# Context rows of the second block made inside the last FFN, keys projected first, late conditioning chunks and gate rows moved

## The reference, cut to what matters

```python
mod  = silu(c)     @ ada_w + ada_b      # sh1, sc1, g1, sh2, sc2, g2
modc = silu(c_ctx) @ ada_w + ada_b      # only sh1c, sc1c are needed
u  = rmsnorm(x,   norm1_g) * (1 + sc1)  + sh1
uc = rmsnorm(ctx, norm1_g) * (1 + sc1c) + sh1c
# token mixer: chunked mLSTM with gates in two directions (q of u; k, v, gates of u and uc),
# then differential attention (q of u; k, v of u and uc), merged with two gates, times w_out
x = x + g1 * y
x = x + g2 * moe_ffn(rmsnorm(x, norm2_g) * (1 + sc2) + sh2)   # 32 experts, top 4
return rmsnorm(x, final_norm_g)
```

## Time and profile before

| what | us |
|---|---|
| median of 3 runs | 2032.08 (2030.83 to 2032.79) |
| profiled execution | 2036.05, its span 2034.3 |
| PE / DVE / ACT busy | 1921.2 / 986.6 / 639.7 |
| POOL busy | 10.3 (24 instructions, nearly all DMA issues) |
| last FFN | about 444 to 632 |
| begin of block 2 to the gates mg | 632 to 685 |
| mLSTM heads | about 744 to 866 |
| attention heads | about 866 to 980 |
| merge, w_out, router | about 980 to 1113 |
| experts | from about 1113 |

### The profile page before, as it was taken

One profiled execution on the slowest core, in us unless ns is written; L12 is line 12 of the kernel. 1 busy time (PEld: TensorE's weight loads), 2 busy tenths in 40 slices (PEclk: granted clock), 3 DMA queues, 4 the chain that ended last, 5 costly groups with the idle time before them and its releaser, 6 DMA issues.

```text
span 2034.3 us, 26514 instructions
## 1 busy us (share of the span) xinstructions
PE 1921.2 (94%) x10854; PEld 1280.8 (63%) x10854; DVE 986.6 (48%) x1679; ACT 639.7 (31%) x1074; POOL 10.3 (1%) x24
## 2 busy tenths in 40 slices
PE   8999999999998998999999999999999888999997
PEld 8979998979997787877897333333333333333332
DVE  6888788878877577666655211111111111111112
ACT  5565556565556332355543100000000000000001
POOL 0000000010000000000000000000000000000000
PEclk9999999999999999999999999999999999999999
DMA  8346554446554542422458999999999999999997
GB/s 339 118 184 222 208 184 169 157 159 261 209 186 166 187 175 104 128 101 83 145 201 328 407 416 431 430 433 433 432 431 430 432 431 431 433 433 432 431 430 309
DMA packets 48621, 590.94 MB, mean 290 GB/s; under 512 B 5584, under 2 KB 6288, under 8 KB 17360
## 3 DMA queue, kind: packets, MB, share of 16 engines
q1 hardware_dynamic: 46752, 584.13, 71.1%
q0 software_dynamic: 1488, 5.28, 0.9%
q10 hardware_dynamic: 288, 0.24, 0.0%
HBM read 588.58 MB, written 1.05 MB: 290 GB/s over the span
## 4 chain that ended last, share of the span: by engine, by line
PE 71%; DMA 19%; DVE 5%; ACT 3%; issue 1%; SPq 0%; DVEq 0%; ACTq 0%
PE psum L2148 44%; PE psum L2598 20%; DMA slots<-exp_w_dram 12%; DMA work<-exp_w_dram 7%; PE psum L2724 3%; PE psum L2543 3%; DVE split_weights L1468 1%; ACT work L994 1%; DVE work L1787 0%; DVE work L1807 0%; DVE cond_work L1461 0%; DVE work L1521 0%; DMA slots<-w_in_dram 0%; ACT split_weights L1044 0%; ACT work L1219 0%
## 5 line engine op out<-in xcount | busy, mean ns | idle before, releaser
L2598 PE MATMUL psum<-slots,work 128*64 128x512 f32 x2304 | 519.0, 603 | 51.4 <-DMA slots<-exp_w_dram 44.1
L2148 PE MATMUL psum<-split_rows,split_weights 128*128 128x256 f32 (+1 forms) x3792 | 509.1, 296 | 8.1 <-DVE split_rows L1428 3.7
L2148 PEld LDWEIGHTS psum<-split_rows,split_weights 128*128 128x128 f32 x3792 | 486.5, 193 | 32.3 <-issue 11.8
L2598 PEld LDWEIGHTS psum<-slots,work 128*64 128x64 f32 x2304 | 168.0, 138 | 365.1 <-issue 331.4
L1449 DVE TENSOR_TENSOR split_weights<-slots,split_weights 128x1024 fp32r<-128x1024 f32 x180 | 219.6, 1224 | 85.5 <-ACT split_weights L1034 84.6
L1034 ACT ACTIVATE split_weights<-slots 128x1024 fp32r<-128x1024 f32 x180 | 190.4, 1062 | 185.7 <-PE psum L2148 165.7
L2148 PE MATMUL psum<-split_weights,split_rows 128*128 128x512 f32 x1008 | 235.3, 393 | 0.0
L2148 PEld LDWEIGHTS psum<-split_weights,split_rows 128*128 128x128 f32 x1008 | 189.2, 189 | 40.4 <-issue 1.3
L2113 DVE TENSOR_SCALAR work<-psum 128x512 f32<-128x512 f32 x32 | 22.0, 688 | 384.0 <-PE psum L2598 384.0
L2598 PE MATMUL psum<-work 128*64 128x512 f32 x768 | 173.1, 603 | 17.6 <-DMA work<-exp_w_dram 17.6
L1357 ACT ACTIVATE work<-work 128x512 f32<-128x512 f32 x32 | 20.2, 631 | 471.6 <-DVE work L2113 471.6
(11 more groups left out here) (286 smaller groups left out, 1418.3 us busy)
## 6 DMA issues: line engine op xcount, KB each, us to landing
slots<-exp_w_dram SPq DMA_DIRECT2D x68, 4096.0 KB, 29.8
work<-exp_w_dram SPq DMA_DIRECT2D x23, 4096.0 KB, 29.8
slots<-w_in_dram SPq DMA_DIRECT2D x56, 1024.0 KB, 5.6
slots<-ffn_up_dram SPq DMA_DIRECT2D x44, 1024.0 KB, 4.9
cond_work<-ada_wT_dram SPq DMA_DIRECT2D x48, 512.0 KB, 4.0
slots<-ffn_down_dram SPq DMA_DIRECT2D x20, 1024.0 KB, 4.9
slots<-w_out_dram SPq DMA_DIRECT2D x12, 1024.0 KB, 4.7
slots<-exp_w_dram SPq DMA_DIRECT2D x4, 2048.0 KB, 9.6
```

Of the source, the lines that this page charges most:

```text
L2148: return nc.tensor.matmul(out_, lhsT, rhs, start=first, stop=last)
L2598: return nc.tensor.matmul(b[rows, :], lhs[:, rows], rhs, start=first, stop=last, skip_group_check=True)
```

## The change

- Context: POOL issues the load of ctx ahead of its other loads. ACT squares its tiles in the first two slots of the last FFN, DVE scales them in slots 4 and 6, PE transposes them in two groups of 8 (ahead of unit "down 4, 0" and ahead of the last two units), ACT evacuates tiles 0 to 2, DVE tile 3, POOL makes the high copies, and DVE makes the four low parts after the first split of block 2 and ahead of the norm's gain.
- Chunks 8 to 15 are loaded and reduced a slot earlier; the first modulation moves to slot 14 and keeps copies of the later bias and gain.
- Units of block 2 begin with mk. PE takes the context half of mk 0 ahead of `keep_clock`, the context half of mk 1 after the transposes of x, then the x halves of both as tiles come ready, then mk 2 and 3, then mq.
- Chunks 16 to 31 are reduced in pairs after units 8 to 15, chunks 32 to 47 one each after units 52 to 67. The second modulation moves behind the merge; PE waits for it ahead of LB.
- `spread` 1 goes behind the second mo slot, 2 and 3 behind the first attention projection; `spread_rows` 1 goes behind the split of unit 26, 2 and 3 ahead of the low part of AT.
- The layout of u puts context and x in two contiguous groups; banks change.

```diff
-B2_SLOTS = [("mq", 0), ("mk", 0), ...
+B2_SLOTS = [("mk", 0), ("mq", 0), ...
-FIRST_COND_UNIT = 4
+COND_UNITS = [8 + i // 2 for i in range(16)] + list(range(52, 68))
...
-B2_BANKS += [("mR", n, 6) for n in range(4)]
+B2_BANKS += [("mR", 0, 6), ("mR", 1, 6)]
...
+B2_BANKS += [("mR", 2, 6), ("mR", 3, 7)]
@@ SP
-                while n_cond[0] < min(len(COND_CHUNKS), 16 + n - FIRST_COND_UNIT + 1):
+                while n_cond[0] < len(COND_CHUNKS) and COND_UNITS[n_cond[0] - 16] <= n:
                     load_cond()
-                    if n >= 9 and n % 2 and n < len(LAYER_SLOTS) - 1:
+                    if 9 - l <= n < len(LAYER_SLOTS) - 1 and ((n + l) % 2 or n == 9) and (l, n) != (1, 9):
                         load_cond()
@@ POOL
             after_evacuation(pool, ("M", 3), DEPTH - 1)
+            pool.dma_start(ctx_row, w["ctx_2"]...).then_inc(ctx_loaded, 16)
...
+            for i in range(4):
+                after_evacuation(pool, ("CT", i), L2)
+                nc.gpsimd.tensor_copy(uT_split[:, 0, 2 * i:2 * i + 2, 0, :], ctx_u_rows[:, i, :]...).then_inc(ctx_high_ready, 1)
@@ ACT
+                def context_work(q, i):
+                    if (l, q, i) == (DEPTH - 1, 15, 2):
+                        context_rows(0)
+                        context_rows(1)
+                    if (l, i) == (DEPTH - 1, 2) and q in (0, 1):
+                        act.wait_ge(ctx_loaded, 16)
+                        nc.scalar.activation(..., ctx_row[:, q, :], ACT.Square, accum_out=...).then_inc(ctx_rms_ready, 1)
+                        act.wait_ge(ctx_rms_ready, q + 1)
+                        if q == 1:
+                            nc.scalar.activation(ctx_rms, ctx_sumsq, ACT.Sqrt, ...).then_inc(ctx_rms_ready, 1)
+                ffn_stages(split_until, first_tap, high_part, context_work)
+                if l == DEPTH - 1:
+                    context_rows(2)
                 splits[l + 1](0)
                 load_root_table()
-                if l == DEPTH - 1:   # wait ctx, two squares, two roots
...
@@ DVE, split2
-                i = 16 + n - FIRST_COND_UNIT
-                if 16 <= i < len(COND_CHUNKS):
-                    conditioning(i, 0)
+                for i, unit in enumerate(COND_UNITS):
+                    if unit == n:
+                        conditioning(16 + i, 0)
@@ DVE, end of the last FFN
                 splits[l + 1](0)
                 if l == DEPTH - 1:
-                    first_modulation()
-                    ...              # reciprocal and scaling of both context tiles
+                    b = take(dve, ("CT", 3), L2)
+                    for c in (0, 1):
+                        ins = nc.vector.tensor_scalar(ctx_u_rows[:, 3, ...], b[...], scale1[...], shift1[...], ALU.mult, ALU.add)
+                    ins.then_inc(evacuated[bank_of(("CT", 3))], 1)
+                    for i in range(4):
+                        dve.wait_ge(ctx_high_ready, i + 1)
+                        nc.vector.tensor_tensor(lo, ctx_u_rows[:, i, :]..., hi, ALU.subtract).then_inc(ctx_u_ready, 1)
@@ DVE, heads and attention
-                spread_rows(1)
-                spread_rows(2)
-                spread_rows(3)
                 for h in range(1, NHM):
...
                     if h == 1:
                         split_until(unit2("dv", 0, 2))
+                        spread_rows(1)
...
                 split_until(next_units(0))
-                dve.wait_ge(cond_done, len(COND_CHUNKS))
-                ...                  # second modulation
+                spread_rows(2)
+                spread_rows(3)
                 low_part_of("AT", a_split, 0)
...
                     y_low_part(2 * g + 1)
...
+                dve.wait_ge(cond_done, len(COND_CHUNKS))
+                nc.vector.tensor_tensor(m, m, late_bias, ALU.add).then_inc(mod2_ready, 1)
+                ...                  # scale2
@@ PE
-                keep_clock(("CT", 0), l, 5)
-                pe.wait_ge(ctx_hat_ready, 1)
-                transposed("CT", l, 0, ctx_row, wait=False)
+                pe.wait_ge(ctx_u_ready, 4)
+                banks = [fill(pe, ("mk", h), l) for h in (0, 1)]
+                units = [next_unit("mk", 0, 0)]
+                key_products(banks[0], units[0], 0, range(KC))
+                keep_clock(("mk", 2), l, 5)
                 transposed("XT", l, 1, wait=False)
+                units.append(next_unit("mk", 0, 1))
+                key_products(banks[1], units[1], 0, range(KC))
+                for k in range(0, KC, 2):
+                    pe.wait_ge(u_ready, k // 2 + 1)
+                    for h in (0, 1):
+                        ins = key_products(banks[h], units[h], 1, (k, k + 1))
...
+                for h in (2, 3):
+                    column_unit(grouped(fill(pe, ("mk", h), l)), "mk", 0, h, u_split)
...                                  # then mq (4 units), mg
-                spread(1)
                 token_rows("mo", 1, (2, 3))
-                spread(2)
+                spread(1)
                 for i in range(8):
                     after_evacuation(pe, ("mv", i), l)
                 m_scores(1)
-                spread(3)
...
                 project_head(0)
+                spread(2)
+                spread(3)
...
                 pe.wait_ge(late_loaded, 32)
+                pe.wait_ge(mod2_ready, 1)
                 b = fill(pe, ("LB", 0), l)
@@ PE, last FFN
+                    if (l, kind, g, j) == (DEPTH - 1, "down", 4, 0):
+                        context_turned((0, 1))
...
+                if l == DEPTH - 1:
+                    context_turned((2, 3))
                 pe.wait_ge(ff_ready, l * 11 + 11)
```

More of the change, by code:

```diff
@@ L524, in build_program @@
         passes = ctx.enter_context(nc.sbuf_tensor("passes", [P, 1], mybir.dt.int32))
-        small = sb("small", 672)
+        small = sb("small", 704)
         small_at = [0]
@@ L757, in ffn_stages @@
                         whole = None
-                    if i == 2 and between and slot < len(LAYER_SLOTS) - 1:
-                        between(slot - 8)
+                    if i in (0, 2) and between:
+                        between(slot - 8, i)
                     if i in (1, 3) and pending is not None:
@@ L1184, in second @@
                 split_until(1)
-                act.wait_ge(scale1_ready, 1)
-                for q in range(8):
-                    key, v, t0, i = ("XT", 0, T, q) if q < 4 else ("CT", 1, 0, q - 4)
+                act.wait_ge(scale1_ready, 2)
+                for i in range(4):
                     if i % 2 == 0:
-                        b = take(act, (key, i), l)
-                        if q >= 4:
-                            act.wait_ge(u_ready, q - 3)
+                        b = take(act, ("XT", i), l)
                         for c in (0, 1):
@@ L1698, in second @@
                 split_until(1)
-                for q in range(8):
-                    key, v, t0, i = ("XT", 0, T, q) if q < 4 else ("CT", 1, 0, q - 4)
+                for i in range(4):
                     if i % 2:
-                        b = take(dve, (key, i), l)
-                        if q >= 4:
-                            dve.wait_ge(u_ready, q - 3)
+                        b = take(dve, ("XT", i), l)
                         for c in (0, 1):
@@ L2261, in column_unit @@
                         for i, (a, v) in enumerate(PASSES):
-                            ins = mm(b, wu[a][:, k, :], rows[v][:, k, t0:], k + i == 0, k == KC - 1 and i == 2)
+                            ins = mm(b, wu[a][:, k, :], rows[v][:, k], k + i == 0, k == KC - 1 and i == 2)
                     item = item_of_unit(n_unit[0] - 1)
@@ L2830, in layer, with context_turned @@
                 turn("F", l, 1)
+                def context_turned(items):
+                    pe.wait_ge(ctx_hat_ready, 2)
+                    for i in items:
+                        b = fill(pe, ("CT", i), L2)
+                        for c in (0, 1):
+                            k = 2 * i + c
+                            for t in range(TT):
+                                ins = nc.tensor.transpose(b[:, c * T + t * P:c * T + (t + 1) * P],
+                                                          ctx_row[:, t, k * P:(k + 1) * P], ident)
+                        done(ins, ("CT", i))
                 for n in range(MIX_UNITS, len(UNITS) - 2):
```

164 lines of the change are left out of this document (93 added, 71 removed).

## The result

The changed kernel takes 2044.58 us (median of 5 runs, 2039.42 to 2046.69), the kernel before 2032.55 (5 runs, 2030.83 to 2036.40). The ratio is 1.0048, with a 95% interval of 1.0036 to 1.0059: slower by half a per cent, where a gain of 3.6 us was forecast. Its profiled execution took 2044.58 (span 2042.8), against 2036.05 (span 2034.3): 8.5 us more.

What follows compares the result with a forecast made beforehand. The experts' weight stream was taken to set the end, by when PE starts it. Terms 7.7 + 0 + 5.2 - 4.9 - 2.8 - 1.6 = 3.6 took 2032.08 to 2028.5; range 2023.3 to 2033.5.

Steps and rivals of the forecast that it cites:

- Part 1: Norm and keys, up to the gates mg: norm's gain 2.3 late, but mg earlier; gain 7.7, between 4.9 and 8.
- Part 2: Start of the FFN: the context lands near 449.6, within the limit of 450.2; cost 0, up to 6 at worst.
- rival B: Norm's chain takes over through POOL's slow copy (2.7) or a late context (3); gain 0.6, 2031.5, chance 0.08.
- Part 3: mLSTM heads: outputs 7.3 earlier, two moved spreads take 2.1 back; gain 5.2, between 4 and 6.
- Part 4: Merge: late chunk loads delay unit 54 and wa; cost 4.9, from 1.3 to 7.
- From there to unit 67 ... level: Merge, behind wa's start: a unit pair gives PE 5.9 and asks DVE 4.6 plus 1 to 2; no further loss.
- Rival C: Units 52 to 67: chunks' round trip paces DVE, eight pairs lose 16.8; sum -8.3, 2040.4, chance 0.08.
- Part 5: LB waits for the second modulation, cost 2.8, plus 1.6 for one clock fall (0 to 3.3).
- The end: Experts' weight stream: the end moves by as much as PE's first expert matmuls, which start that stream.

Runs made afterwards that it cites:

- Run 9: The changed kernel with the 32 chunks at units 4 to 35, one each, as in the kernel before; ratio 1.0011 to the kernel before.
- run 5: The changed kernel with SP issuing each late chunk's load one unit earlier; ratio 1.0012 to the kernel before.
- run 13: The changed kernel with POOL's two late loads (0.66 MB) held until BT is evacuated; ratio 1.0065 to the kernel before.
- run 1: The changed kernel with ACT's two context squares and their load wait in the last FFN's second slot; median 2043.66, ratio 1.0047 to the kernel before.
- run 10: The changed kernel with constant matmuls in PE's waits, 8 ahead of unit 54 and 4 ahead of LB; median 2044.12, ratio 1.0048 to the kernel before.
- run 2: The changed kernel with the last 16 chunks moved from the merge to units 16 to 19 and 27 to 35; ratio 1.0000 to the kernel before.

## Why the prediction was wrong, step by step

- **Part 1, norm and keys: right.** 7.7 forecast, 7.9 measured, by the steps named: mg was due at 677.6, and with the 4.3 lost in the FFN 681.9 is its place to a tenth. The gain came 2.4 late (forecast 2.3). POOL's copies took 0.61 to 0.75 alone (0.63 was taken from ACT's row), and the last one 2.21 for the reason above.
- **Part 2, the context's load: wrong.** "Alone in front, with one issue and a start of 4.9 ... it lands near 449.6" was the step that failed. It looked at the seven loads of POOL's own queue. What the context shared the engines with were SP's five halves, issued from 433.8 on. They stand in the trace of before too, and bytes over 420 GB/s would have given 452 from it. The worst landing was in the text (456.5) and rival B had 3 us at a chance of 0.08 for it and POOL together; that was too low. Of the 4.3 that it cost, 1.5 were slow matmuls behind the wait, which the text had in no term for this place.
- **Part 3, heads: right.** 7.3 and 7.3; the spreads cost 1.8, forecast 2.1. Run 9 puts the chunks' share at 3.2, where the text had 2.3, so the sum's tenth is partly luck.
- **Part 4, chunks in the merge: right in kind, mis-sized.** This is the term that failed by most, 12.6 for 4.9. The places were the ones named (ahead of unit 54, ahead of wa), but they cost 8.0 + 1.7, not 4.9. Chunk 33's landing was taken as 6.8 and was 8.8, and the stall it made 5.4 and not 2.8. The fall of the clock behind the stall (2.6, and 1.0 in wa) was charged once, for LB. With the FFN's 1.5 and LB's 1.6 the slow matmuls come to 6.7 us, where the sum had 1.6. And "From there to unit 67 ... level" was wrong: y's gating and low part were counted as 1 to 2 of merging, with ACT's share they are 2.7, and the second group lost 2.9, 1.0 of it the clock in wa.
- **Rival C was half of the mechanism.** The chunks' round trip did stand on the chain, with five loads of 4.7 to 8.8. But C had a loss of 2.1 in each of eight pairs, and DVE's idle was 7.3 on two loads and 0.1 to 0.8 on the other five; with the loads early (run 5) the second group still lost 3.0, to DVE's own work. It got 0.08, with the argument that only four of 48 landings were long. Their median there was 4.7 and not the 3.6 to 4.0 of the earlier trace rows, and C's own point of decision was 4.7. That C's sum of -8.3 is so near to the measured -8.0 is luck: it had 16.8 for the merge, which cost 12.6, and nothing for the context's load, which cost 4.3. That this comes from the halves issued right ahead of them is argued from the order on SP's queue; only POOL's share was measured (run 13).
- **Part 5, LB: right.** 4.4 forecast, 4.4 measured, 2.8 of stall and 1.6 of clock. In the seven kernels whose LB waits 3.10, that stage lies 4.4 to 7.1 over 63.1, so 1.6 for the fall was the cheap end, and the hit to a tenth is partly luck.
- **The end: right.** It moved with the mark (8.5 and 8.1). From the mark to the end all fifteen profiles lie between 917.8 and 923.2.

**Open:** in three kernels (changed, 1 and 13) the first expert matmuls came at 1121.3, though runs 1 and 13 stood 5.1 and 5.5 us earlier at BT. What they gave back behind BT is more slow clock than wait, at other places in each; that it comes out to a tenth may be chance. Why the clock falls behind some idles and not behind others of the same length isn't known.

## What to carry to other kernels

Add up the bytes that are in flight on all queues when a load is issued, and divide by the rate at full use: for the context this gave 452.2, and it landed at 453.1, while a median over calmer stretches does not tell it. It is a lower bound: for chunk 33, POOL's bytes explain 1.6 of the 3.2 us that they cost. A small load with two buffers in a stretch where its consumer is in the critical order is a chain of round trips, and what a repair of one link wins can be lost at the next (runs 10 and 13). Issuing all the late chunks' loads a unit earlier won 8.2 us of the merge (run 5); taking the work out of the stretch won all 12.6 (run 2), for nothing in exchange. Where a stall of PE is priced, price the slow matmuls behind it with it, at each place.

## What the runs showed of the hardware

- POOL's 0.66 MB beside a chunk put its landing off by 3.2 us (8.8 against 5.6, one execution of each kernel), though the bytes alone are 1.6 us at 420 GB/s.
- The granted clock fell behind many idles of PE of 2.3 to 6 us, to the lower level (1.2 GHz) for a while; the price was 1.0 to 4.3 us, and not the same for the same idle (LB: 3.10 idle in seven kernels, last stage 67.5 to 70.3, where 63.1 and the stall's 2.8 would be 65.9). Behind others it did not fall: 3.35 in the FFN of run 5 (216 matmuls in 26.17, clock 1.00), 2.80 in its merge (144 in 17.51).
- It fell with PE busy too, at matmuls of 4 columns (14 of them in 2.49 against 1.71, granted clock 0.67 in that stretch against 1.00); that alone moved the heads' stage by 1.6 to 3.2 us between kernels that are alike there. With matmuls of constants through the wait it did not fall (6.02 against 8.56).
- Beside three of DVE's instructions with two SBUF inputs, POOL's copy grew from 0.61 to 2.21 us, while these were not slowed.
